# One slab of weights between the steps of a gated linear attention, and another order of a kernel's first loads

## The reference, cut to what matters

```python
# one layer of the first block, for each stream (x: latent, hctx: context)
x  = x + 0.5*mx[2]*swiglu(ada_norm(x, norm_g[l,0], mx[0], mx[1]), ffn_w_in[l,0], ffn_w_out[l,0])
hx = ada_norm(x, norm_g[l,1], mx[3], mx[4])
y  = even_mixer(...) if l % 2 == 0 else odd_mixer(...)
x  = x + mx[5]*y
x  = x + 0.5*mx[8]*swiglu(ada_norm(x, norm_g[l,2], mx[6], mx[7]), ffn_w_in[l,1], ffn_w_out[l,1])
```

## Time and profile before

| | us |
|---|---|
| three runs | 3312.4, 3300.83, 3307.23 |
| median | 3307.23 |
| profiled execution, its time | 3309.09 |
| its span in the profile | 3307.3 |
| TensorE busy | 2942.9 (89% of the span) |
| VectorE busy | 1943.7 (59%) |
| ScalarE busy | 1186.6 (36%) |

### The profile page before, as it was taken

How to read it: one execution, slowest core, us unless ns; L and a number is a source line. 1 busy time by engine, 2 the same in 40 slices (tenths; PEclk the granted TensorE clock), 3 DMA queues, 4 the chain that set the end, 5 groups by cost and what they waited for, 6 DMA issues and landing times.

```text
span 3307.3 us, 38261 instructions
## 1 busy us (share of the span) xinstructions
PE 2942.9 (89%) x15162; PEld 2392.6 (72%) x15162; DVE 1943.7 (59%) x3133; ACT 1186.6 (36%) x1950; POOL 558.8 (17%) x579
## 2 busy tenths in 40 slices
PE   0999998988899999999995789979889998988797
PEld 0788886544788888888883589955678777854797
DVE  5887854544677857787534466543356665433554
ACT  2322233343422233222325355434352223425452
POOL 1000010321100010000101010103341113125431
PEclk9999998987999999999996699999989999989898
DMA  6455522101355534555230045420123442232453
GB/s 234 159 204 202 184 77 76 51 26 39 121 198 203 203 104 173 195 207 181 90 132 13 1 142 189 153 71 26 64 102 140 147 161 94 102 69 27 130 183 109
DMA packets 125282, 412.14 MB, mean 125 GB/s; under 512 B 25088, under 2 KB 27136, under 8 KB 124464
## 3 DMA queue, kind: packets, MB, share of 16 engines
q1 hardware_dynamic: 107824, 346.78, 31.2%
q0 software_dynamic: 17280, 62.92, 5.5%
HBM read 408.60 MB, written 1.05 MB: 124 GB/s over the span
## 4 chain that ended last, share of the span: by engine, by line
PE 79%; DVE 8%; ACT 7%; issue 2%; POOL 2%; DMA 1%; SPq 0%; POOLq 0%; ACTq 0%; DVEq 0%
PE bank L2066 24%; PE bank L2068 23%; PE bank L2067 23%; PE bank L2255 1%; POOL sb_temp L1094 1%; DVE sb_temp L1622 1%; DVE sb_split_low L1608 1%; PE bank L2216 1%; PE bank L2387 1%; DVE sb_rstd L1664 1%; DVE sb_temp L1672 1%; PE bank L2245 1%; PE bank L2334 1%; ACT sb_split_high L1236 1%; PE bank L2386 1%
## 5 line engine op out<-in xcount | busy, mean ns | idle before, releaser
L2066 PE MATMUL bank<-sb_h_high,sb_split_high 128*128 128x256 f32 (+1 forms) x3048 | 1062.3, 349 | 131.6 <-DVE sb_h_low L1678 75.9
L2067 PE MATMUL bank<-sb_h_low,sb_split_high 128*128 128x256 f32 (+1 forms) x3048 | 1041.7, 342 | 0.0
L2068 PE MATMUL bank<-sb_h_high,sb_split_low 128*128 128x256 f32 (+1 forms) x3048 | 1040.7, 341 | 0.0
L1608 DVE TENSOR_TENSOR sb_split_low<-sb_raw,sb_split_high 128x1024 fp32r<-128x1024 f32 x515 | 636.9, 1243 | 256.8 <-ACT sb_split_high L1236 252.5
L2066 PEld LDWEIGHTS bank<-sb_h_high,sb_split_high 128*128 128x128 f32 x3048 | 591.5, 194 | 222.1 <-issue 89.9
L1236 ACT ACTIVATE sb_split_high<-sb_raw 128x1024 fp32r<-128x1024 f32 x515 | 535.6, 1050 | 376.9 <-DMA sb_raw<-weights 376.9
L2067 PEld LDWEIGHTS bank<-sb_h_low,sb_split_high 128*128 128x128 f32 x3048 | 594.2, 195 | 67.4 <-issue 0.5
L2068 PEld LDWEIGHTS bank<-sb_h_high,sb_split_low 128*128 128x128 f32 x3048 | 592.8, 194 | 67.3
L1622 DVE CUSTOM_DVE_ANT_0 sb_temp<-sb_ada_ffn,sb_cond_ffn 128x1024 bf16<-128x1024 f32 x408 | 479.2, 1219 | 28.4 <-DMA sb_ada_ffn<-ada 28.2
L1728 DVE SCALAR_TENSOR_TENSOR sb_x_res<-bank,sb_gates,sb_x_res 128x256 f32<-128x256 f32 x288 | 129.4, 478 | 290.7 <-PE bank L2068 290.2
L2066 PE MATMUL bank<-sb_hidden_high_ffn,sb_split_high 128*128 128x512 f32 (+1 forms) x788 | 272.7, 346 | 0.0
(11 more groups left out here) (246 smaller groups left out, 3292.8 us busy)
## 6 DMA issues: line engine op xcount, KB each, us to landing
sb_raw<-weights SPq DMA_DIRECT2D x515, 512.0 KB, 3.3
sb_ada_ffn<-ada SPq DMA_DIRECT2D x102, 512.0 KB, 4.2
sb_ada_ffn<-ada POOLq DMA_DIRECT2D x102, 512.0 KB, 3.6
sb_ada_mlp<-ada SPq DMA_DIRECT2D x18, 512.0 KB, 4.2
sb_ada_mlp<-ada POOLq DMA_DIRECT2D x18, 512.0 KB, 4.2
sb_cond_ffn<-cond SPq DMA_DIRECT2D x3, 1024.0 KB, 5.6
sb_na_raw<-na_rpb SPq DMA_DIRECT2D x32, 96.0 KB, 5.8
sb_x_res<-tokens SPq DMA_DIRECT2D x1, 2048.0 KB, 14.4
```

What stands on the lines that cost most here:

```text
L1608: do.tensor_tensor(m.low[i][:, :], m.raw[i][:, :], m.high[i][:, :].bitcast(F32), ALU.subtract).then_inc(*dve.mark("split_low", s))
L2066: do.matmul(out, ah, bh, start=start and j == 0, stop=False)
L2067: do.matmul(out, ah, bl, start=False, stop=False)
L2068: last = do.matmul(out, al, bh, start=False, stop=stop and j == len(terms) - 1)
```

## The change

1. **Odd mixer.** The step functions `gla_*` now handle both directions at once. A head is seven steps: keys, scores, state with inner, and four chunks; at each of them stands a part of the next head's decays (`gla_factors` of the next head with chunk 1) or of the previous head's output (`swish` and `gla_norm` with chunk 2). Behind each of the 28 steps comes at most one piece: in the first 21 steps the second half of the values (8 pieces), the gates r (8 pieces, 5 gaps), and in the last 7 steps the first half of `odd_out`, which is now cut in two halves over its inputs. Ahead of the heads stand the rank, the queries and the first half of the values, with the decays of head 0 between them. The factors have two sets of buffers, by the head's parity, in parts of the odd memory that nothing else uses. The recurrence uses banks 0 to 3, the pieces 4 and 5. The head's output is written into the context half of h, so that the pieces can still read the latent half.
2. **First loads.** SP issues the condition vectors first, then `ada` 0 to 5, then tables, constants and tokens; all 24 first `ada` go through SP. The first seven slabs are fetched behind `ada` 9 to 15. Slab 0 is split behind `ada` 15, slabs 1 to 4 among the tiles of the first norm.
3. **First squares.** TensorE adds the squares of `n00` up in PSUM, one product with ones for each of 16 tiles (`first_square`), in place of 14 additions on POOL and two products; the tiles, and `mean` (VectorE, ScalarE, VectorE) for both streams, stand in the list behind `ada` 12.
4. **Lambda** moves from the even mixer to the start, behind `ada` 23 and the gates of the first layer, with a scratch that fits there.
5. **Squares of the even mixer.** TensorE's part is a step of its own, `sum_squares`, one unit behind ScalarE's.

```diff
-    out["odd_out"] = slabs(f("odd_w_out")[0], 8)
+    out["odd_out"] = half_slabs(f("odd_w_out")[0], (0, 1))
...
-    yield from weave(mv, [[("conv", 0)], [("conv", 1)], [("conv", 2)], [("conv", 3)], [("forget", 0)], [("forget", 1)], [("lambda",)]])
+    yield from weave(mv, [[("conv", 0)], [("conv", 1)], [("conv", 2)], [("conv", 3)], [("forget", 0)], [("forget", 1)]])
...
-        extra[at] = [("add_squares", "ml", j)]
+        extra[at] = extra[at] + [("add_squares", "ml", j)]
+        extra[at + 1] = extra[at + 1] + [("sum_squares", "ml", j)]
...
+def gla_steps(hd):
+
+    out = hd > 0
+    more = hd + 1 < 4
+    tag = ("gla", hd - 1)
+    yield [("gla_keys", hd)] + [("gla_out", hd - 1)] * out + [("gla_decay0", hd + 1, 1, 3)] * more
+    yield [("gla_scores", hd)] + [("gla_square", hd - 1)] * out + [("gla_decay1", hd + 1)] * more
+    yield [("gla_state", hd), ("gla_inner", hd)] + [("gla_sum", hd - 1)] * out + [("gla_decay2", hd + 1)] * more
+    yield [("gla_chunk", hd, 0)] + [("mean", tag, LAT_PART)] * out + [("gla_decay3", hd + 1)] * more
+    yield [("gla_chunk", hd, 1)] + [("gla_factors", hd + 1)] * more
+    yield [("gla_chunk", hd, 2)] + [("swish", hd - 1), ("gla_norm", hd - 1)] * out
+    yield [("gla_chunk", hd, 3)]
+
+
+def odd_steps():
+
+    ring = Ring(0, 6)
+    yield from fm_pieces("odd_rank", ring)[1][0]
+    groups = [[("gla_decay0", 0, 4, 5)], [("gla_decay1", 0)], [("gla_decay2", 0)], [("gla_decay3", 0)], [], [("gla_factors", 0)]]
+    first = Ring(0, 4)
+    yield from weave(fm_pieces("odd_q", first)[1] + list(tm_pieces("odd_tm", first, 0)), groups)
+    ring = Ring(4, 2)
+    r = fm_pieces("odd_r", ring)[1]
+    pieces = list(tm_pieces("odd_tm", ring, 1)) + r[:4] + [None, r[4], None, r[5], None, r[6], None, r[7], None, None]
+    outs = [out_piece("odd_out", k, 0, LAT_PART, ring) for k in range(DT)]
+    steps = [step for hd in range(4) for step in gla_steps(hd)]
+    yield from beside([(step, []) for step in steps[:21]], pieces)
+    yield from beside([(step, []) for step in steps[21:]], outs)
+    yield "gla_out", 3
+    yield "gla_square", 3
+    yield from flat(outs)
+    yield "gla_sum", 3
+    yield "mean", ("gla", 3), LAT_PART
+    yield "swish", 3
+    yield "gla_norm", 3
...
-    yield "inputs",
...
-    for k in range(DT):
-        for p in (0, 1):
-            yield "square", "n00", k, p
-    for n in range(16):
+    for n in range(ADA_SLOTS):
         yield "ada", n
+    yield "inputs",
+    for n in range(ADA_SLOTS, 16):
+        yield "ada", n
+        if n >= 16 - SLOTS:
+            yield "fetch", n - 16 + SLOTS
+        if n == 12:
+            for p in (0, 1):
+                for k in range(DT):
+                    yield "first_square", "n00", k, p
+                yield "mean", "n00", p
+    yield "split", 0
     yield "mods", 0, 16
     yield "scales", "n00"
-    yield from flat(ada_norm_groups("n00", 0))
-    yield from weave(head[0], ada_norm_groups("n00", 1))
+    first, *tiles = ada_norm_groups("n00", 0)
+    yield from weave([[("split", s)] for s in range(1, SLOTS - LAG)], tiles)
+    first, *tiles = ada_norm_groups("n00", 1)
+    yield from weave(head[0], tiles)
     for n in range(16, 24):
         yield "ada", n
     yield "mods", 16, 8
     yield "gates", "ffn00"
+    yield "lambda",
...
     def squared(tag, k, p):
 
-        if k >= 2:
+        if k >= 2 and tag == "n00":
+            act.wait_ge("summed", ("first", k - 2, p))
+        elif k >= 2:
             act.wait_ge("added", ("square", tag, max(k - 2, 1), p))
...
+    def gla_decay1(hd):
+        la, tmp = [gla_tiles(m, d)[0] for d in range(2)], [gla_tiles(m, d)[1] for d in range(2)]
+        for d in range(2):
+            act.wait_ge("decay_act", (0, hd, d))
+            do.activation(tmp[d], la[d], ACT.Abs).then_inc(*act.mark("decay_act", (1, hd, d)))
+        for d in range(2):
+            act.wait_ge("decay_act", (1, hd, d))
+            do.activation(tmp[d], tmp[d], ACT.Exp, scale=-1.0).then_inc(*act.mark("decay_act", (2, hd, d)))
+        for d in range(2):
+            act.wait_ge("decay_act", (2, hd, d))
+            do.activation(tmp[d], tmp[d], ACT.Ln, bias=1.0).then_inc(*act.mark("decay_act", (3, hd, d)))
...
 def chunk_bank(d, n):
-    return 3 * d + (1, 2, 0)[n]
+    return 2 * d + (1, 0, 1)[n]
```

More of the change, by code:

```diff
@@ L787, in schedule @@
 def schedule():
-    for s in range(SLOTS):
-        yield "fetch", s
-    for s in range(SLOTS - LAG):
-        yield "split", s
     for step in order():
@@ L1083, in ada @@
     def ada(n):
-        if n % 2 == 0:
+        if n % 2 == 0 and n >= 24:
             load_ada(m, pool, n)
@@ L1501, in gla_out, with gla_keys @@
+    def gla_keys(hd):
+        for d in range(2):
+            act.wait_ge("keys_turned", (hd, d))
+            do.activation(m.gla_kt[d][:, :], m.bank[2 * d][:, :], identity).then_inc(*act.mark("keys_copy", (hd, d)))
     def gla_out(hd):
@@ L2085, in add_up, with first_square @@
         do.matmul(m.bank[bank][:, 0:NC_TOK], m.C("ones"), m.acc[:, COLS[p]], start=True, stop=True).then_inc(*pe.mark("summed", key))
+    def first_square(tag, k, p):
+        pe.wait_ge("inputs", "all")
+        pe.wait_ge("squared", (tag, k, p))
+        do.matmul(m.bank[6 + p][:, 0:NC_TOK], m.C("ones"), m.squares[k % 2][:, COLS[p]], start=k == 0, stop=k == DT - 1).then_inc(
+            *pe.mark("summed", ("first", k, p), (tag, p)))
+        read[6 + p] = "mean", (tag, p)
     def sum_of_squares(tag, p):
-        pe.wait_ge("inputs", "all")
         pe.wait_ge("added", ("square", tag, DT - 1, p))
@@ L2324, in gla_state, with gla_scores @@
[L2324 to L2331 removed]
+    def gla_scores(hd):
+        for d in range(2):
+            bank = 2 * d + 1
+            pe.wait_ge("factor_dve", ("k", hd, d))
+            free(bank)
+            for tile in range(2):
+                c = slice(tile * P, (tile + 1) * P)
+                last = do.matmul(m.bank[bank][:, c], gla_qk(m, hd, d, 1)[:, c], gla_qk(m, hd, d, 0)[:, c], start=True, stop=True)
+            last.then_inc(*pe.mark("inner_scored", (hd, d)))
+            read[bank] = "inner_masked", (hd, d, 1)
```

413 lines of the change are left out of this document (208 added, 205 removed).

## The result

The changed kernel takes 3183.65 us (median of four runs, 3181.99 to 3187.15) where the kernel before took 3307.07 beside it: a ratio of 0.9632, 95% interval 0.9617 to 0.9646. That is 123 us less, where 111 was forecast (3198, range 3160 to 3245).

What follows compares the result with a forecast made beforehand. TensorE, busy for 89% of the span, was taken as the bound, with latencies between engines in the odd mixer's heads. Gains of 16.4 + 10.5 + 11 + 73 = 111 us from 3309.1 gave 3198 us, range 3160 to 3245.

Steps and rivals of the forecast that it cites:

- The forecast case: Whole kernel: start 16.4, even mixer 10.5, squares 11 and odd mixer 73 us gained, giving 3198 us; chance 0.58.
- First loads: Start: condition vectors first bring slab 16's first dot 20.3 us earlier, despite a new VectorE wait of 7 us.
- Lambda: Its move costs 3.9 us at the start and lets TensorE resume some 10.5 us earlier in the even mixer.
- Squares: Even mixer: seven of eight TensorE waits for squares get cover; 13.4 us, taken as 11 (bounds 3 and 14).
- Ahead of the heads: Odd mixer: rank, decays, q and half-value pieces run from 1654.4 to 1694.7, with head 0's 23 us of decays beside them.
- The heads: Odd mixer's four heads: 139.5 us against 135.4 before, no shorter, but with 23 pieces inside.
- The waits on copies: Odd mixer: TensorE waits for bank 4's copy, 3.5 us in head 0 and 7.8 us in head 1.
- Tail and last halves: Odd mixer's end: a tail of 9.9 plus 0.3 us, then eight output halves, 12 us in place of 22.
- The first rival: Odd mixer's clock stays low: heads take 200 us, not 139.5; gain 51, time 3258; chance 0.12.
- The second: Rival: copies behind the chain cost nothing and the latent squares are quick; gain 137, time 3172; chance 0.20.
- The third: Rival: pieces and recurrence block each other at every step of the odd mixer's heads; time 3351; chance 0.04.
- The fourth: Rival: the start gains nothing, as the modulation's transfers in one queue come too slowly; time 3214; chance 0.06.

Runs made afterwards that it cites:

- the old order inside the heads: Against the run without pieces (3193.12 us): sum and mean ahead of decays, directions unpaired, factors at the front of their own head; 3217.38 us, ratio 0.9723.
- the kernel in which they do cost nothing: Changed kernel with the copies of the piece before put ahead of the step's own work at steps 5 and 9; 3172.38 us, ratio 0.9592.
- the old start: Changed kernel with the order of first loads, the first squares and the modulation slabs' queues as in the kernel before; 3204.36 us, ratio 0.969.

## Why the prediction was right, and where it was not

The forecast case came in, all four parts near their size, but its largest part (80.2 where 73 was predicted) is right in size for partly wrong reasons. All parts behind the start came out larger than predicted.

- *First loads*: predicted 20.3 at slab 16, measured 18.3. First dot 8.09 for 7.4, stall of `ada 6` 0.21 for 1, VectorE's wait 5.34 for 7. The new wait behind the first `mean` was there, and moving the means removed it.
- *Lambda*: -3.9 at the start, measured 3.9 by putting it back; +10.5 in the even mixer, measured 12.0 between the two kernels and 11.4 by the edit.
- *Squares*: 11, measured 13.6. I had kept 2.4 us for waits that come back; 4.4 did, so that fewer waits gave 9.1; another 4.5 came of TensorE's busy time, which my sum didn't have. That two misses of opposite sign leave a number so near is luck. The one wait for squares that is left is 2.1, predicted 2.2.
- *Ahead of the heads*: 40.3, measured 41.7. That head 0's decays are hidden was right, and is worth 20 us.
- *The heads*: 139.5 predicted, 129.0 measured. The step that was off is "TensorE's own work at full clock I take as busy time times granted clock": 15.0 + 16.4 + 16.4 + 14.6 = 62.4. The heads without pieces give by the same product 13.2, 13.1, 13.4 and 12.5, that is 52.2. The 10.2 between them is nearly the size of the miss of 10.5, but not every term beside it fits: the heads came out 1.9, 1.5, 1.5 and 5.6 us below the forecast, the waits on copies were 3.8 shorter than predicted, and head 3, where I had allowed 2.4 us for a low clock, ran at 1.00. The products hold for the old order inside the heads too (12.8, 13.7, 13.4 and 12.4), so it isn't the order of the chains that made them smaller. The rows of before held one direction's products behind the other's; I carried this busy time over as if it belonged to the work, though the change puts the two side by side.
- *The waits on copies*: 3.5 and 7.8 us, measured 2.52 and 5.00, at the two places named. Removing them gave 10.5 to 11.3, since the clock rose too.
- "The heads get no shorter, but 8 value, 8 r and 7 half-output pieces are inside": this reading credits the pieces. The run without them shows that the heads had become 48 us shorter by themselves, and that laying 23 pieces inside brought 9.5 on top. In my sum both went into one number, and only the total was tested. I had every row for the other reading: the waits for the state copy behind eight activations and four table loads, and the exposed factors.
- *Tail and last halves*: 10.5 and 12.5 for 10.2 and 12.
- A slip in the working: for a clock of 0.6 throughout, the bound is given as 15, but the rival's own 200 us for the heads leave 73 - 60.5 = 12.5. Nothing else rests on it.
- *The clock*: above 0.8 in heads 0 and 1, as said (0.95, 0.87). The first rival is refuted. The second, that the copies cost nothing, is refuted in its reason; the kernel in which they do cost nothing takes 3172. That this is the rival's number too is chance: its sum had the latent squares quick as well, and in that kernel they aren't. The third, pieces and recurrence blocking each other at every step, did not come up: beside the two waits on copies, none inside the heads was over 2.21 us. The fourth is refuted by the old start.

Where the odd mixer's 80.2 us came from, by the runs: head 0's decays beside products about 20; the pieces 9.5; the order of sum, decays and factors with the pairing 20 to 24, measured without pieces (beside pieces the pairing alone costs 6.2 and the place of the factors alone 4.0); the directions' products side by side some 14, by rows alone. These terms needn't add up exactly. The 12 us or so of the heads that are left are, by the estimates above, 8 us of a higher granted clock in the same work, 2.5 us of less work in other groups and 1.7 us of waits; no edit shows these shares.

## What to carry to other kernels

- Before crediting overlap, time the chain alone: a kernel with the pieces taken out from between the steps told in one run that a shorter chain had brought 48 us and the filling 9.5 on top. The filling's worth holds for the chain that it was tried beside.
- Busy time times clock is the work of an engine in its present order only. If a change reorders the instructions, look whether neighbours use all rows of the array.
- In a shared list of steps, put what frees a bank or feeds a split ahead of the long chain on its engine, and anything that waits for another engine (a mean, a lambda) behind whatever is ready.

## What the runs showed of the hardware that was not expected

- Float32 matmuls of 64 rows whose operands lie in opposite halves of the partitions run at the same time when issued next to each other: four in 1.23 us, two in 1.22, both at the lower clock; at the higher one the next instruction starts 0.63 us after the first of two and of four.
- A wait of TensorE costs more than its length: 7.5 us of waits removed gave 10.5, with busy time 1.8 us shorter in each of two heads (granted clock 0.95 to 1.00, and 0.87 to 0.95). After 15.7 idle us the same head took 40.9 us in place of 36.5.
- Changing between Exp and Ln cost 1.28 us each time. The Trainium skill (ScalarE: Activation LUTs, "Table sets: the hidden batching unit") has a set with both; the rows show that the loads were there all the same.
